# Reading the moving tile backwards, and writing the accumulator backwards, in the block products of a float32 transformer kernel

## The reference, cut to what matters

```python
def first_block(x, ...):
    z = modulate(rmsnorm(x, norm1_g), sh1, sc1) @ w_in          # 1024 x 2560
    y = concat([head_rmsnorm(y_a), head_rmsnorm(y_b)]) @ w_out
    x = x + g1 * y
    h = modulate(rmsnorm(x, norm2_g), sh2, sc2)
    x = x + g2 * peer(h, w_q, sub_keys, expert_u, expert_v)     # u and v: 16384 x 1024 each
    return rmsnorm(x, final_g)

def second_block(x, ...):
    h = x + hybrid_mixer(rms_norm(x, norm_mix_g), ...)          # w_in_2, w_branch, w_out_2
    h = h + (silu(hn @ w_gate) * (hn @ w_up)) @ w_down          # 1024 x 2816, twice, and back
    return rms_norm(h, norm_final_g)
```

## Time and profile before

| | |
|---|---|
| median of 2 runs | 2518.4 us (2516.34 to 2520.46) |
| profiled execution, own time | 2516.58 us |
| its span, first to last instruction | 2515.2 us |
| mean granted TensorE clock | 0.99 of full speed |
| TensorE busy with matmuls | 2456.2 us, 98% of the span, 11288 records |
| weight loads (overlap the matmuls) | 2023.0 us, 80% |
| VectorE, ScalarE, GpSimd busy | 63%, 35%, 30% |

### The profile page before, as it was taken

The page is one execution under the profiler, slowest core; times in us unless marked ns, Lnnn a source line. Parts: engine busy times, 40 slices in busy tenths (PEclk is TensorE's granted clock), DMA queues, the critical chain, the costliest instruction groups (busy, mean ns, idle before and its releaser), DMA issues.

```text
span 2515.2 us, 29977 instructions
## 1 busy us (share of the span) xinstructions
PE 2456.2 (98%) x11288; PEld 2023.0 (80%) x11288; DVE 1577.4 (63%) x3102; ACT 884.8 (35%) x1362; POOL 761.3 (30%) x473
## 2 busy tenths in 40 slices
PE   6999999999999999999999999999999989999998
PEld 3778878888778888888888888888888778888887
DVE  6675698679996883445665555554676547444333
ACT  4433432333334333233333333334445543322221
POOL 1434227776877670000000000004333332111100
PEclk9989999999999999999999999999999999999999
DMA  7656666666676775346464555534232343332332
GB/s 273 211 182 210 176 177 144 140 143 176 143 185 151 193 176 201 113 159 226 167 227 166 209 184 185 208 101 130 85 115 88 98 163 96 97 99 95 92 105 80
DMA packets 189190, 388.02 MB, mean 154 GB/s; under 512 B 47148, under 2 KB 114860, under 8 KB 181296
## 3 DMA queue, kind: packets, MB, share of 16 engines
q1 hardware_dynamic: 147928, 324.88, 40.4%
q0 software_dynamic: 41120, 61.23, 10.0%
HBM read 312.72 MB, written 70.98 MB: 153 GB/s over the span
## 4 chain that ended last, share of the span: by engine, by line
PE 68%; DVE 3%; ACT 1%; DMA 1%; issue 0%; ACTq 0%; POOLq 0%
PE bank L526 19%; PE bank L530 19%; PE bank L527 19%; PE bank_stat L879 1%; PE bank_stat L880 1%; PE bank_stat L884 1%; DVE hot_weight L1931 1%; PE bank L762 1%; PE bank L911 1%; PE bank L909 1%; PE bank L924 1%; PE bank L677 1%; DVE weights_lo L1572 1%; PE bank_stat L552 0%; PE bank L543 0%; PE bank L544 0%
## 5 line engine op out<-in xcount | busy, mean ns | idle before, releaser
L526 PE MATMUL bank<-h_lo,weights_hi 128*128 128x512 f32 x2204 | 865.9, 393 | 8.3 <-DVE gates L2200 3.8
L527 PE MATMUL bank<-h_hi,weights_hi 128*128 128x512 f32 x2204 | 862.6, 391 | 0.0
L1063 ACT ACTIVATE weights_hi<-weights_raw 128x1024 fp32r<-128x1024 f32 (+1 forms) x411 | 432.8, 1053 | 418.2 <-PE bank L530 313.9
L530 PE MATMUL bank<-h_hi,weights_lo 128*128 128x512 f32 x2204 | 547.3, 389 | 2.6 <-DVE weights_lo L1572 2.6
L1572 DVE TENSOR_TENSOR weights_lo<-weights_raw,weights_hi 128x1024 fp32r<-128x1024 f32 x351 | 443.0, 1263 | 103.7 <-ACT weights_hi L1063 89.0
L2376 POOL DMA_INDIRECT expert_coefs<-share,place_at x256 | 442.0, 1727 | 194.8 <-issue 95.1
L526 PEld LDWEIGHTS bank<-h_lo,weights_hi 128*128 128x128 f32 x2204 | 416.5, 189 | 95.6 <-DVE gates L2200 3.9
L530 PEld LDWEIGHTS bank<-h_hi,weights_lo 128*128 128x128 f32 x2204 | 413.6, 188 | 90.4 <-DVE weights_lo L1572 4.5
L527 PEld LDWEIGHTS bank<-h_hi,weights_hi 128*128 128x128 f32 x2204 | 416.4, 189 | 85.0 <-issue 0.2
L1789 DVE SCALAR_TENSOR_TENSOR residual<-bank,ada,residual 128x512 f32<-128x512 f32 x135 | 101.5, 752 | 313.8 <-PE bank L530 313.8
L1274 ACT ACTIVATE hidden<-bank 128x512 f32<-128x512 f32 x128 | 76.6, 598 | 455.6 <-PE bank L530 447.9
(11 more groups left out here) (405 smaller groups left out, 2894.1 us busy)
## 6 DMA issues: line engine op xcount, KB each, us to landing
weights_raw<-in_expert_u SPq DMA_DIRECT2D x128, 512.0 KB
weights_raw<-in_expert_v SPq DMA_DIRECT2D x128, 512.0 KB
weight<-expert_coefs POOLq DMA_DIRECT2D x16, 2048.0 KB, 8.5
hidden_store<-hidden SPq DMA_DIRECT2D x26, 1024.0 KB
hidden<-hidden_store POOLq DMA_DIRECT2D x13, 2048.0 KB, 14.5
ada_raw<-in_w_ada SPq DMA_DIRECT2D x34, 512.0 KB, 6.5
expert_coefs<-zeros SPq DMA_DIRECT2D x32, 512.0 KB, 6.3
expert_coefs<-stage SPq DMA_DIRECT2D x16, 1024.0 KB, 6.1
```

The lines of the kernel that those rows point to most:

```text
L526: M.matmul(bank[:], hi[:, c:c + P], m_lo[k], start=start and i == 0, stop=False)
L527: M.matmul(bank[:], hi[:, c:c + P], m_hi[k], start=False, stop=False)
L530: ins = M.matmul(bank[:], lo[:, c:c + P], m_hi[k], start=False, stop=stop and i == len(tiles) - 1)
L1063: S.activation(w_hi[n % SPLIT][:, 0:w], w_raw[n % RAW][:, 0:w], ACT.Copy).then_inc(*hi_done.inc(n))
```

## The change: the direction of two access patterns

In `partial`, the moving tile is given as `m[k][:, ::-1]`, so that token 511 enters first and token 0 last, and the accumulator as `bank[:, ::-1]`, so that the first result lands in column 511. Each token's result is still added into its own column. Number, size, order and operands of the instructions, their waits and all other lines are as before; on no engine does an instruction stand elsewhere in the program.

```diff
                     if ready:
                         for done in ready(k):
                             M.wait_ge(*done)
-                    M.matmul(bank[:], hi[:, c:c + P], m_lo[k], start=start and i == 0, stop=False)
-                    M.matmul(bank[:], hi[:, c:c + P], m_hi[k], start=False, stop=False)
+                    M.matmul(bank[:, ::-1], hi[:, c:c + P], m_lo[k][:, ::-1], start=start and i == 0, stop=False)
+                    M.matmul(bank[:, ::-1], hi[:, c:c + P], m_hi[k][:, ::-1], start=False, stop=False)
                 M.wait_ge(*lo_done(n))
                 for i, (c, k) in enumerate(tiles):
-                    ins = M.matmul(bank[:], lo[:, c:c + P], m_hi[k], start=False, stop=stop and i == len(tiles) - 1)
+                    ins = M.matmul(bank[:, ::-1], lo[:, c:c + P], m_hi[k][:, ::-1], start=False, stop=stop and i == len(tiles) - 1)
```

## The result

The changed kernel took 2570.18 us (median of 2 runs, 2568.89 to 2571.47) against 2518.4 us: a ratio of 1.0206, with a 95% interval of 1.0162 to 1.0249. The forecast was no change. The time lies inside the range, but not at the likeliest case: it is nearest to the third rival, a small price for each changed matmul, at 52 of its 118 us.

The account below looks back on a forecast made before the run. The prediction took TensorE, busy 98% of the span, as the bound; every term of the reversal was put at 0, so 2516.58 us + 0 = 2517 us, set at the median, 2518 us, with a range of 2508 to 2636 us.

Parts of the forecast that it names:

- no change: Whole kernel: the reversed direction is free and the time stays at 2518 us; the likeliest case, chance 0.69.
- the third rival: Each changed product matmul: a small fixed price of up to 13 ns, 2636 us at the top; chance 0.11.
- a fixed price: Start of each product matmul: 13 ns fixed part, bounded from -118 to +118 us, taken as 0.
- a price of the column: Each product matmul's columns: at least today's 0.417 ns, added time 0 or 1843 us with nothing between; taken as 0.
- half rate: Backward pattern served every second cycle: 203 ns more for each of 9078 product matmuls, 1843 us; chance 0.17.
- The bound: Product lines on TensorE: each nanosecond added to or taken from one matmul moves the time by 9.1 us, hidden by nothing.
- the second rival: Array input or accumulator of the product matmuls slower by half the streaming rate: 4350 to 4361 us; chance 0.17.
- handing over banks: ScalarE and VectorE wait for a block's last matmul as a whole, never for a column: 0 us.
- adding into a bank backwards: Consecutive matmuls of a block, all backward, rewrite every column at the same distance as forwards: 0 us.
- the granted clock: Sign in the changed kernel's profile: should stay at 0.99; lower would mean something other than the pattern's rate.

Follow-up runs that it names:

- within_16_back: Probe kernel of thirteen reading orders: one group of 192 expert_v matmuls reads the moving tile backwards inside groups of 16 tokens, groups taken forwards; spacing 266.7 ns.
- the kernel with both: The changed kernel (tile and accumulator backwards) with the split weights also 64 bytes earlier; 2570.66 us, ratio 1.0204.
- the probe: Kernel before, with weight tiles read 0 to 112 columns earlier in thirteen expert_v groups (tile forwards) and twelve expert_u groups (tile backwards); forwards 226.6 ns at 64 columns.

## Why the prediction was wrong

The step that failed is the price of one matmul. The prediction took it as a sum of two terms and put both at 0: a fixed price, "since the fixed part is that of starting one matmul behind another, which the change leaves alone", and a price of the column, since "nothing lies between them by mechanism", that is between no price and a half rate. What the runs showed in its place is +6.6 ns for each backward read of 512 columns, times 9078, all of it on the read of the moving tile.

The reason given for the fixed price is refuted. The 13 ns are not the cost of a start that nothing else touches: with every pattern forwards, the place of the two tiles against each other by 256 bytes moves the 226.7 ns to 229 and up to 233. The reason given for the column's price isn't borne out either. Between the two sizes a backward column costs 0.449 ns, less than a tenth more than 0.417, and within_16_back has a spacing of 266.7 ns, which lies between the full and the half rate. How the 6.6 ns divide between the two terms stays open; the size of their sum is what the runs give.

One reading of the numbers, which isn't proved, is that the change added no cost but lost a discount. At 512 columns the median spacing of a backward read stayed at 233 to 234 ns at every weight place and width tried, while the forward read has 226.7 only where its 128 weight columns lie well against it, and 228 to 233 elsewhere. The two causes don't add, as the kernel with both shows.

The bound was sound. The prediction asked for 9.1 us for each nanosecond, since nothing hides TensorE; 6.6 ns made 60 us of busy time and 55.0 us of span, 8.3 us for each, because some 5 us of TensorE's own waits shrank.

The evidence that the prediction brought against the small price was read too widely. The second half of a tile follows at the same 120 ns as the first, which is true, but 256 columns are a multiple of the period of 64; the tile shifted by 32 costs 232 ns. And the 393 ns of `merged_lo` stood in the earlier trace rows and weren't taken up.

The price of the half rate was too small as well. It was taken from the durations of a plain float32 matmul, 203 ns more, though such a matmul leaves two records and the duration is that of one. The order that did halve the rate here, every second column, cost 453 - 226.7 = 226 ns more from start to start, by which the second rival would be an estimated 2518 + 2054 = 4572 us and not 4361. That the half rate didn't come leaves this without effect on the result; that the time fell into the range was owed to the bound of the third rival, not to the reason for the forecast.

What held: a backward read isn't at half the rate (0.17 in the chances); handing over banks and adding into a bank backwards cost nothing, shown by the run that writes backwards alone; the granted clock stayed at 0.99. The strict reading of the Trainium skill, "Advanced Engine Details and Errata", "PSUM Cachelines", that any non-contiguous pattern slows matmuls significantly, doesn't hold for a step of -1: 0.9997. Its "SBUF Cachelines" asks for at least two hits on a line of 16 bytes. For these float32r reads two weren't enough: two columns a line had 453 ns, and four in the orders tried inside the line 226.7.

Still open: the mechanism. That the forward spacing depends on the place of the two tiles against each other is shown; that two reads collide somewhere in the buffer's memory is only argued, and that a shorter weight load made the forward matmuls slower speaks against its simplest form. Why a backward read of 512 columns has about 233.3 ns whatever the weights do, why at 256 columns it is the faster one, and why within_16_back has 33 ns more than backwards isn't explained.

## What to carry to other kernels

In a kernel that TensorE bounds, the order and the place of its operands are worth a check even when the instructions are the same: 64 bytes in the allocation of the weights cost 0.65% here and turning the read round 2%. For float32r matmuls of 128 weight columns by 512 tokens, as here, let the addresses of the moving and the stationary tiles differ by a multiple of 256 bytes and run forwards through each 64 columns. The order of these stretches, the order inside 16 bytes and the direction of the accumulator were free. A "fixed part" found by comparing two sizes is a leftover, not a constant: before taking it as unaffected, look for a row in which it differs, as `merged_lo` did here.

## What the runs showed of the hardware that was not expected

- For 512 float32r columns the spacing was 226.7 ns in the best placement. The place of the tiles alone made it up to 233 ns forwards and up to 238.5 backwards; no group of any order or place went below 226.6.
- The two tiles' places count against each other, and the pattern repeats after 256 bytes: weights 64 bytes off 229.0 ns in the whole program, 64 columns off 226.6 in the probe.
- Matmuls of 256 columns are the other way round: backwards 118.3 ns on average, forwards 120.0, and 32 us less for the whole program cut into halves (one run each).
- Reading each group of 16 tokens backwards and the groups forwards cost 266.7 ns, more than reading everything backwards (233.3).
- Taking every second column, or every second pair, cost 451 to 453 ns: half the rate, though the accumulator was written in order.
- With only one weight column to load, the load lasted 82 ns and the forward matmuls were spaced wider (231.3 ns) than with 128.
